# Long filters of block 2 made in eight parts between its first products, by position parity, kept in DRAM and read back

## The chip, the cores and the metric

The kernel runs on one core of a Trainium2 chip. TensorE multiplies matrices into the accumulators (PSUM), VectorE and ScalarE do the element-wise work, GpSimd (POOL) here only takes a few inverse roots, and SyncE (SP) issues the DMAs that bring weights from DRAM. The engines run side by side and meet at semaphores. The metric is the time of one execution on the device in microseconds (us), less is better.

## The reference

Two blocks are run one after the other on 256 positions of 2048 channels, in float32. The change touches the second block's mixer, and there the long filters. They depend on the weights alone, not on the input:

```python
def hyena_kernel_fft(L, fw1, fb1, freq, fw2, fb2, fw3):
    ...
    hdn = jnp.sin(freq * (feats @ fw1 + fb1))
    hdn = jnp.sin(freq * (hdn @ fw2 + fb2))
    h = (hdn @ fw3).astype(f32).reshape(L, HY_ORDER, 2, HY_W)
    ...
    h = h * jnp.exp(-t[:, :, None, None] * jnp.abs(deltas))
    k = jnp.concatenate([h[:, :, 0], jnp.zeros((1, HY_ORDER, HY_W), f32), h[:0:-1, :, 1]], axis=0)
    k = k / (jnp.sum(jnp.abs(k), axis=0, keepdims=True) + EPS)
    return jnp.fft.rfft(k, axis=0)
...
    for o, gate in enumerate(gates):
        z = gate * (fft_conv(z, kf[:, o]) + z * lp['hy_bias'][o])
```

L is 256, HY_W is 1024. `fft_conv` transforms z, multiplies by the filter's spectrum and transforms back. The kernel does the transforms as matmuls with tables of cosines and sines at the odd frequencies, since the sum of both halves of the filter gives the real part and their difference the imaginary one.

## The kernel before

Everything is float32. A weight piece is 512 x 512, arrives in two DMAs (halves of 512 KB) in one of four ring slots (`w_raw`), is split by ScalarE into a high part (`w_hi`, line 1039 in block 2) and by VectorE into the rest (`w_lo`, line 1662), and TensorE multiplies it in three passes (lines 2359 to 2361, `product2`). A product with one stream is 24 matmuls of 512 columns. Piece n can be loaded when product n - 4 is done; each engine's code splits piece n + 2 in iteration n.

Block 2 starts with the 12 chunks of its input projection (loop `for j in range(12)`). Chunks 0 to 3 are made for two streams, x and the context c. Chunk 0 has pieces 0 to 3, first with c and then with x, since x comes last out of block 1: between its products TensorE turns the normalised x (`turn_x2`), VectorE modulates it (`whole`), ScalarE rounds it (`whole_hi`) and VectorE takes the rest. Chunk 1 has products 4 to 7, chunk 2 has 8 to 11, chunk 3 (`DT`) is product 12 and the first x-only chunk starts at 13. At the end of a chunk ScalarE copies the accumulators out (line 1127) before the next chunk can write them. Between the products stand the short convolutions: TensorE turns a tile forward, ScalarE and VectorE apply the taps (`centre2`, `taps2`), TensorE turns it back. All orders are written out by hand: the order of the code of an engine is its order of work. `side` is a pair of accumulator banks and `turn` another, each handed over by a full and a free semaphore, in the order of the lists `side_uses` and `order`.

Behind the last chunk come the scan's heads (until about 2533 us of the span), its output (VectorE lines 1862 to 1872), and then, in this order on TensorE:

- the filters, for each of the two orders: the taps `h` (line 2583, 8 matmuls of 512 columns on 64 rows), their norm (line 2590, 8 matmuls with ones on `h_abs`, which ScalarE makes), and the spectra `K` of sum and difference (line 2599, 16 matmuls). VectorE applies the decay (lines 1885, 1887), sums (1890, 1892), takes the reciprocal of the norm (1906) and scales the spectra (1913);
- the convolutions, for each order and each half c of the channels: forward transform `Z` (line 2617), VectorE's product with `K` (lines 1926 to 1934), inverse transform into `side` (line 2628), and VectorE's bias, add and gate (lines 1941 to 1947). Between the first two transforms the gate rows are spread (`spread_gate`, line 2605);
- the output projection. Its weights from the third piece on are loaded when the convolutions are done, because their slots hold `hy_b`, `fw3` and `idft` until then.

## Time and profile before

| | us |
|---|---|
| median of 3 runs | 3564.24 (3562.53 to 3570.66) |
| profiled execution, its own time | 3575.23 |
| its span | 3573.4 |
| TensorE busy in the span | 3451.4 |
| VectorE busy | 2355.6 |
| ScalarE busy | 1617.9 |

The profile is one execution, recorded by the hardware. "Busy" is the time in which an engine worked on an instruction; matmuls are pipelined, so their shown durations overlap and the distance from start to start is what one costs. PEclk is the clock that TensorE was granted, as a share of 2.4 GHz; the clock has two levels, 1.2 and 2.4 GHz, so a window with 0.75 was at each for half of the time. A name such as `L2617` is the line of the kernel before. Each float32 matmul of the filters and convolutions shows as two records (x16 are 8 matmuls); those of the products are one each.

### The profile page before, as it was taken

To read this page: it belongs to the slowest core of one execution; us is meant where nothing else is said; L and a number is where in the kernel's file an instruction comes from. 1 tells how busy PE (TensorE), PEld (TensorE's weight loads), DVE (VectorE), ACT (ScalarE), POOL (GpSimd) and SP (SyncE) were. 2 spreads that over 40 slices of the span, in tenths; PEclk is the share of its full clock that TensorE was granted. 3 is DMA by queue.
4 is the path that set the end of the run, shared out by engine and by line. 5 is a ranking of instruction groups with operands and counts; after the bars stand their busy time and mean duration, and the time that the engine had idled before them with its cause. 6 is when DMAs were issued, how large, how long until landed. Compare 5 with 4: busy or idle time off the path is not lost.

```text
span 3573.4 us, 42859 instructions
## 1 busy us (share of the span) xinstructions
PE 3451.4 (97%) x15810; PEld 2810.8 (79%) x15810; DVE 2355.6 (66%) x2911; ACT 1617.9 (45%) x2131; POOL 33.4 (1%) x28
## 2 busy tenths in 40 slices
PE   7999999999999999999999999999887999999998
PEld 6888888887788888888878887878534788888887
DVE  5667888888766666777767663566655665656565
ACT  5555555555434545555554442444211543434343
POOL 0000000000000000000000000000000000000000
PEclk9999999999999999999999999999988999999999
DMA  7557777776676467777777753566002576667664
GB/s 237 151 175 221 225 220 226 227 229 213 224 238 205 142 188 227 226 226 230 231 220 256 252 173 96 155 195 195 1 0 96 160 221 201 220 200 222 201 220 157
DMA packets 357809, 687.84 MB, mean 192 GB/s; under 512 B 24591, under 2 KB 28704, under 8 KB 356384
## 3 DMA queue, kind: packets, MB, share of 16 engines
q1 hardware_dynamic: 357664, 685.82, 61.1%
q8 instruction: 101, 1.65, 0.2%
q14 instruction: 44, 0.36, 0.0%
HBM read 683.64 MB, written 2.10 MB: 192 GB/s over the span
## 4 chain that ended last, share of the span: by engine, by line
PE 69%; issue 21%; DVE 5%; ACT 2%; DMA 1%; DVEq 1%; SPq 0%; ACTq 0%; POOL 0%; POOLq 0%
PE acc L2083 16%; PE acc L2085 16%; PE acc L2084 16%; PE acc L2359 4%; PE acc L2360 4%; PE acc L2361 4%; DVE w_lo L1247 1%; DMA w_raw<-in_w_down 1%; PE turn L2290 1%; PE acc L2617 1%; PE turn L2104 1%; PE turn L2120 1%; PE acc L2583 1%; DVE ada_sum L1350 1%; PE side L2628 1%
## 5 line engine op out<-in xcount | busy, mean ns | idle before, releaser
L1247 DVE TENSOR_TENSOR w_lo<-w_raw,w_hi 128x1024 fp32r<-128x1024 f32 x708 | 838.4, 1221 | 380.4 <-ACT w_hi L771 346.2
L771 ACT ACTIVATE w_hi<-w_raw 128x1024 fp32r<-128x1024 f32 x708 | 739.0, 1062 | 718.2 <-DMA w_raw<-in_w_up 315.3
L2083 PE MATMUL acc<-w_hi,in_h 128*128 128x512 f32 x1408 | 553.0, 393 | 0.0
L2085 PE MATMUL acc<-w_hi,in_l 128*128 128x512 f32 x1408 | 548.6, 390 | 0.0
L2084 PE MATMUL acc<-w_lo,in_h 128*128 128x512 f32 x1408 | 548.0, 389 | 0.0
L2022 DVE TENSOR_TENSOR w_lo<-w_raw,w_hi 128x1024 fp32r<-128x1024 f32 x252 | 303.1, 1222 | 195.7 <-ACT w_hi L1211 187.6
L1211 ACT ACTIVATE w_hi<-w_raw 128x1024 fp32r<-128x1024 f32 x252 | 264.7, 1060 | 330.2 <-DMA w_raw<-in_w_mlp 329.8
L2359 PE MATMUL acc<-w_hi,in_h 128*128 128x512 f32 x992 | 395.9, 399 | 15.9 <-issue 6.0
L2361 PE MATMUL acc<-w_hi,in_l 128*128 128x512 f32 x992 | 390.3, 393 | 0.0
L2360 PE MATMUL acc<-w_lo,in_h 128*128 128x512 f32 x992 | 390.2, 393 | 0.0
L1350 DVE SCALAR_TENSOR_TENSOR ada_sum<-w_raw,silu_c,ada_sum 128x512 f32<-128x512 f32 x450 | 327.6, 750 | 31.7 <-issue 8.0
L2083 PEld LDWEIGHTS acc<-w_hi,in_h 128*128 128x128 f32 x1408 | 264.4, 188 | 56.2 <-issue 1.6
L2085 PEld LDWEIGHTS acc<-w_hi,in_l 128*128 128x128 f32 x1408 | 264.2, 188 | 55.6
L2084 PEld LDWEIGHTS acc<-w_lo,in_h 128*128 128x128 f32 x1408 | 264.5, 188 | 53.4
L2083 PE MATMUL acc<-w_hi,ah 128*128 128x512 f32 x704 | 278.9, 396 | 14.2 <-DVE w_lo L1247 7.5
L2084 PE MATMUL acc<-w_lo,ah 128*128 128x512 f32 x704 | 276.3, 392 | 0.0
L2085 PE MATMUL acc<-w_hi,al 128*128 128x512 f32 x704 | 276.2, 392 | 0.0
L2359 PEld LDWEIGHTS acc<-w_hi,in_h 128*128 128x128 f32 x992 | 188.6, 190 | 58.5 <-issue 17.3
L2361 PEld LDWEIGHTS acc<-w_hi,in_l 128*128 128x128 f32 x992 | 188.5, 190 | 40.3
L2360 PEld LDWEIGHTS acc<-w_lo,in_h 128*128 128x128 f32 x992 | 188.8, 190 | 38.2 <-issue 0.5
L2359 PE MATMUL acc<-w_hi,hid_h 128*128 128x512 f32 x512 | 200.4, 391 | 0.0
L2361 PE MATMUL acc<-w_hi,hid_l 128*128 128x512 f32 x512 | 199.4, 389 | 0.0
(353 smaller groups left out, 4730.1 us busy)
## 6 DMA issues: line engine op xcount, KB each, us to landing
w_raw<-in_w_up SPq DMA_DIRECT2D x352, 512.0 KB, 3.8
w_raw<-in_w_mlp SPq DMA_DIRECT2D x256, 512.0 KB, 3.7
w_raw<-in_w_in SPq DMA_DIRECT2D x200, 512.0 KB, 3.7
w_raw<-in_w_ada SPq DMA_DIRECT2D x192, 512.0 KB, 4.2
w_raw<-in_w_down SPq DMA_DIRECT2D x176, 512.0 KB, 4.8
w_raw<-in_w_o SPq DMA_DIRECT2D x64, 512.0 KB, 3.7
w_raw<-in_w_out SPq DMA_DIRECT2D x32, 512.0 KB, 3.8
x_sb<-in_x SPq DMA_DIRECT2D x1, 2048.0 KB, 7.8
```

The costliest lines, as they stand in the source:

```text
L771: nc.scalar.activation(hi[s][:, ks], raw[s][:, ks], ACT.Copy).then_inc(w_hi[s][h], 1)
L1211: nc.scalar.activation(hi[s][:, 2 * h:2 * h + 2], raw[s][:, 2 * h:2 * h + 2], ACT.Copy).then_inc(w_hi[s][h], 1)
L1247: nc.vector.tensor_tensor(lo[s][:, ks], raw[s][:, ks], hi[s][:, ks].bitcast(F32), ALU.subtract).then_inc(w_lo[s][h], 1)
L1350: a = nc.vector.scalar_tensor_tensor(ada_sum[v][:], raw[s][:, k], c, ada_sum[v][:], ALU.mult, ALU.add)
L2022: nc.vector.tensor_tensor(lo[s][:, ks], raw[s][:, ks], hi[s][:, ks].bitcast(F32), ALU.subtract).then_inc(w_lo[s][h], 1)
L2083: nc.tensor.matmul(acc[p][i][:], high(kt)[:, tok], hi[s][:, k], start=(kt == first), stop=False)
L2084: nc.tensor.matmul(acc[p][i][:], high(kt)[:, tok], lo[s][:, k], start=False, stop=False)
L2085: last = nc.tensor.matmul(acc[p][i][:], low(kt)[:, tok], hi[s][:, k], start=False, stop=(kt == final))
L2104: last = nc.tensor.transpose(tb[b][:, i * P:(i + 1) * P], src, ident[:])
L2359: nc.tensor.matmul(o, h_[:, kt, tok], wh[:, k, 0:cols], start=(kt == first), stop=False)
L2360: nc.tensor.matmul(o, h_[:, kt, tok], wl[:, k, 0:cols], start=False, stop=False)
L2361: last = nc.tensor.matmul(o, l_[:, kt, tok], wh[:, k, 0:cols], start=False, stop=(kt == final))
```

## The change

The filters no longer stand behind the scan. They are made in eight steps, of one order and 256 channels each, and each step has two visits of TensorE between products of block 2's first chunks:

- the first visit, in a slot of `FLT_A`, makes both directions' taps into the two banks of `side` (4 matmuls of 256 columns). VectorE then applies the decay and makes sum and difference (`filter_taps`). The norm's argument |a| + |b| is taken as the larger of |a + b| and |a - b|, on VectorE;
- the second visit, in a slot of `FLT_B`, makes the norm (2 matmuls, into `turn`) and the transform (4 matmuls). The positions are sorted into even and odd ones, and the frequencies into a first half and its mirror image, so one half table (`fdft`, 128 columns) gives two partial sums, and the spectrum's halves are their sum and difference, which VectorE makes (`filter_spectrum`). The order's bias is added to the real part there, so that the convolution's result needs the gate alone.

Slot -4 to -1 are behind chunk 0's products with c, slot n is behind product n. The slots are `FLT_A = [-4, -1, 2, 4, 6, 8, 10, 12]` and `FLT_B = [-3, 0, 3, 5, 7, 9, 11, 13]`. A step's spectra (0.5 MB) are stored to a DRAM tensor; when the projection's last pieces are used up, all are read back to where the weights of the ring's two free slots were, in pieces of 1 KB in a partition's row. VectorE waits for them at the first product of each order.

Also moved: the two small matmuls and sines that make `hdn` (from the chunk at product 28 on to the last down projection of block 1), the loads of `dft`, `masks` and the filter's small weights (to the same place), the modulation of x (from VectorE to ScalarE, `whole_features`), and the normalisation of the scan's output (from the middle of the filters to behind VectorE's products of the first order). Buffers were given other addresses.

The diff, cut to its core:

```diff
+    by_parity = np.concatenate([pos[0::2], pos[1::2]])
+    c["feats"] = np.concatenate([t, np.cos(f * w), -np.sin(f * w)], 1).T.astype(f32)[:, by_parity].copy()
...
+    freq = np.concatenate([pos[:P], pos[::-1][:P]])
+    ang = 2 * np.pi * ((2 * freq[None, :] + 1) * pos[:, None] % (4 * TOK)) / (4 * TOK)
+    c["fdft"] = np.stack([v[by_parity, 0:P].astype(f32).reshape(TT, P, P).transpose(1, 0, 2) for v in (np.cos(ang), np.sin(ang))], 1).copy()
...
+        def filter_load(s):
+
+            o, ch = s // 4, slice(s % 4 * FC, (s % 4 + 1) * FC)
+            sp.wait_ge(flt_taps, s)
+            w3 = t["filt_w3_2"][0].rearrange("k (o d n) -> k o d n", o=2, d=2)
+            sp.dma_start(flt_w[:], w3[:, o, :, ch]).then_inc(flt_in, 16)
+            sp.dma_start(flt_decay[:], t["decay"][:, :, ch]).then_inc(flt_in, 16)
+            sp.dma_start(flt_b[s % 2][:], t["hy_bias_2"][:, o, ch].to_broadcast([P, FC])).then_inc(flt_in, 16)
+
+        def filter_store(s):
+
+            sp.wait_ge(k_made, s + 1)
+            sp.dma_start(k_store[s, :, 0], flt_sum[:]).then_inc(k_stored, 16)
+            sp.dma_start(k_store[s, :, 1], flt_dif[:]).then_inc(k_stored, 16)
+
+        def filter_moves(n):
+
+            for s in range(8):
+                if n == max(3, FLT_A[s] + 5) and s < 7:
+                    filter_load(s + 1)
+                if n == max(3, FLT_B[s] + 5):
+                    filter_store(s)
+
+        sp.wait_ge(sin_s, 2)
+        filter_load(0)
         for j, (col, _, _) in enumerate(CHUNKS):
             if j == DT:
                 s, r = ring(FIRST[j])
...
+                sp.wait_ge(w_free[ring(OUT0 + n)[0]][h], ring(OUT0 + n)[1])
+        sp.wait_ge(k_stored, 16 * 16)
         for o in range(2):
-            sp.dma_start(fw3[o][:], t["filt_w3_2"][0][:, o * 2 * HYW:(o + 1) * 2 * HYW]).then_inc(fw3_in, 16)
-        sp.dma_start(idft[:], t["idft"]).then_inc(idft_in, 16)
+            for m in range(2):
+                for q in range(4):
+                    sp.dma_start(K[o][m][:, :, q * FC:(q + 1) * FC], k_store[4 * o + q, :, m]).then_inc(k_in, 16)
+            if o == 0:
+                sp.dma_start(idft[:], t["idft"]).then_inc(idft_in, 16)
...
+        def whole_features(names, full, dst):
+
+            for i, u in enumerate(names):
+                b, k = UNITS[u]
+                act_.wait_ge(t_full[b], k)
+                for f in range(2):
+                    kt = 2 * i + f
+                    src, s_, b_ = tb[b][:, f * TOK:(f + 1) * TOK], scale2[:, 0, kt:kt + 1], mod[:, kt, 0:1]
+                    nc.scalar.activation(full[:, kt], src, ACT.Identity, scale=s_, bias=b_)
+                    a = nc.scalar.activation(dst[:, kt], src, ACT.Identity, scale=s_, bias=b_)
+                a.then_inc(part2_hi, 1)
+                act_.drain().then_inc(t_free[b], 1)
...
+        def filter_taps(s):
+
+            for b in range(2):
+                dve.wait_ge(side_full[b], SIDE[b]["h", s] + 1)
+            two = lambda b: side[b][:].rearrange("p (t n) -> p t n", t=TT)
+            nc.vector.tensor_tensor(flt_h0[:], two(0), flt_decay[:], ALU.mult).then_inc(side_free[0], 1)
+            nc.vector.scalar_tensor_tensor(flt_q[:, 0], two(1)[:, 0], not_first[:], flt_decay[:, 0], ALU.mult, ALU.mult)
+            nc.vector.tensor_tensor(flt_q[:, 1], two(1)[:, 1], flt_decay[:, 1], ALU.mult).then_inc(side_free[1], 1)
+            dve.drain()
+            if s > 0:
+                dve.wait_ge(k_stored, 32 * s)
+            nc.vector.tensor_tensor(flt_sum[:], flt_h0[:], flt_q[:], ALU.add)
+            nc.vector.tensor_tensor(flt_dif[:], flt_q[:], flt_h0[:], ALU.subtract)
+            dve.drain()
+            nc.vector.tensor_tensor(flt_q[:], flt_sum[:], flt_dif[:], ALU.max)
+            nc.vector.tensor_tensor(flt_h0[:], flt_sum[:], flt_dif[:], ALU.min)
+            dve.drain()
+            nc.vector.scalar_tensor_tensor(flt_q[:], flt_h0[:], -1.0, flt_q[:], ALU.mult, ALU.max)
+            dve.drain().then_inc(flt_taps, 1)
+
+        def filter_spectrum(s):
+
+            b, k = UNITS["nm", s]
+            dve.wait_ge(t_full[b], k)
+            nc.vector.tensor_scalar(flt_r[:], tb[b][:, 0:FC], EPS, None, ALU.add).then_inc(t_free[b], 1)
+            dve.drain()
+            nc.vector.reciprocal(flt_r[:], flt_r[:])
+            dve.drain()
+            for m, dst in enumerate((flt_q, flt_h0)):
+                dve.wait_ge(side_full[m], SIDE[m]["dft", s] + 1)
+                nc.vector.tensor_tensor(dst[:], side[m][:].rearrange("p (t n) -> p t n", t=TT),
+                                        flt_r[:].unsqueeze(1).to_broadcast([P, TT, FC]), ALU.mult).then_inc(side_free[m], 1)
+            dve.drain()
+            nc.vector.tensor_tensor(flt_q[:, 0], flt_q[:, 0], flt_b[s % 2][:], ALU.add)
+            nc.vector.tensor_tensor(flt_dif[:, 0], flt_h0[:, 0], flt_h0[:, 1], ALU.add)
+            nc.vector.tensor_tensor(flt_dif[:, 1], flt_h0[:, 1], flt_h0[:, 0], ALU.subtract)
+            dve.drain()
+            nc.vector.tensor_tensor(flt_sum[:, 0], flt_q[:, 0], flt_q[:, 1], ALU.add)
+            nc.vector.tensor_tensor(flt_sum[:, 1], flt_q[:, 0], flt_q[:, 1], ALU.subtract)
+            dve.drain().then_inc(k_made, 1)
+
+        def filter_step(slot):
+
+            if slot in FLT_A:
+                filter_taps(FLT_A.index(slot))
+            if slot in FLT_B:
+                filter_spectrum(FLT_B.index(slot))
+
+        for i in range(8):
+            if i % 2 == 0:
+                filter_step(i // 2 - 4)
+            dve.wait_ge(part2_hi, 8 + i + 1)
+            two = slice(2 * i, 2 * i + 2)
+            nc.vector.tensor_tensor(in_l[:, two], in_f[:, two], in_h[:, two].bitcast(F32), ALU.subtract).then_inc(part2_lo, 1)
...
-            dve.wait_ge(filt_in, 16 * 8)
-            dve.wait_ge(t_full[b], k)
-            nc.vector.tensor_scalar(hdn_a[:], tb[b][0:HY_HID, 0:TOK], filt[:, i + 1:i + 2], filt[:, 0:1], ALU.add, ALU.mult).then_inc(t_free[b], 1)
-            dve.drain()
...
-            for c in range(2):
-                nc.vector.tensor_scalar(r_norm[:, c * CH:(c + 1) * CH], side[c][:], EPS, None, ALU.add).then_inc(side_free[c], 1)
-            dve.drain()
-            nc.vector.reciprocal(r_norm[:], r_norm[:])
-            dve.drain()
+            dve.wait_ge(k_in, 128 * (o + 1))
...
@@ -1935,17 +1985,19 @@
                     if m == 1:
                         a.then_inc(yf_s, 1)
                     dve.drain()
+            if o == 0:
+
+                dve.wait_ge(ssd_sq, 1)
+                nc.vector.tensor_scalar(ss2[:, 0, 0:4], ss2[:, 0, 0:4], 1.0 / 512, EPS, ALU.mult, ALU.add).then_inc(stat, 1)
+                dve.wait_ge(rstd, 19)
+                y_groups = xs[0][:].rearrange("p t (g w) -> p (t g) w", w=CH)
+                nc.vector.tensor_tensor(y_groups, y_groups, rstd2[:, 0, 0:4].unsqueeze(2).to_broadcast([P, 4, CH]), ALU.mult).then_inc(mix_s, 1)
             for c in range(2):
                 ch = slice(c * CH, (c + 1) * CH)
-                dve.drain()
-                nc.vector.tensor_tensor(hy_t[:], hy[0][:, :, ch], hy_b[:, o, ch].unsqueeze(1).to_broadcast([P, TT, CH]), ALU.mult)
-                dve.drain()
                 for i in range(TT):
                     dve.wait_ge(side_full[i], SIDE[i]["conv", o, c] + 1)
-                    nc.vector.tensor_tensor(hy_t[:, i], hy_t[:, i], side[i][:], ALU.add).then_inc(side_free[i], 1)
-                dve.drain()
-                nc.vector.tensor_tensor(hy[0][:, :, ch], hy_t[:], hy[1 + o][:, :, ch], ALU.mult).then_inc(conv_s, 1)
-                dve.drain()
+                    nc.vector.tensor_tensor(hy[0][:, i, ch], side[i][:], hy[1 + o][:, i, ch], ALU.mult).then_inc(side_free[i], 1)
+                dve.drain().then_inc(conv_s, 1)
         nc.vector.tensor_tensor(hy_sq[:], hy[0][:], hy[0][:], ALU.mult)
...
+        def filter_visit(slot):
+
+            if slot in FLT_A:
+                s = FLT_A.index(slot)
+                if s == 0:
+                    pe.wait_ge(ada_mod, 2 * ADA_LAYER + 1)
+                pe.wait_ge(flt_in, 48 * (s + 1))
+                for d in range(2):
+                    o = fill_side(d, ("h", s))
+                    for tt in range(TT):
+                        last = nc.tensor.matmul(o[:, tt * FC:(tt + 1) * FC], hdn[1][:, tt * P:(tt + 1) * P], flt_w[:, d], start=True, stop=True)
+                    last.then_inc(side_full[d], 1)
+            if slot in FLT_B:
+                s = FLT_B.index(slot)
+                pe.wait_ge(flt_taps, s + 1)
+                b = fill(("nm", s))
+                for tt in range(TT):
+                    last = nc.tensor.matmul(tb[b][:, 0:FC], masks[:, ONES], flt_q[:, tt], start=(tt == 0), stop=(tt == 1))
+                last.then_inc(t_full[b], 1)
+                for m, src in enumerate((flt_sum, flt_dif)):
+                    o = fill_side(m, ("dft", s))
+                    for tt in range(TT):
+                        last = nc.tensor.matmul(o[:, tt * FC:(tt + 1) * FC], fdft[:, m, tt], src[:, tt], start=True, stop=True)
...
+                filter_visit(n)
```

In the diff of VectorE's part the lines left out ahead of `dve.wait_ge(k_in, ...)` are the whole of the old filter code (lines 1874 to 1915), and on TensorE lines 2577 to 2600 go.

On TensorE, behind the scan's output, the rows of the kernel before end the second order's filters and come to the first convolution (`hy` is z, `dft_sb` the table):

```order
L2575 MATMUL side<-states,bcT 128x512 x8
L2583 MATMUL acc<-fw_0_243,hdn_220 128x512 x8
L2590 MATMUL side<-h_abs_201,masks_sb 128x512 x4
L2590 MATMUL side<-h_abs_202,masks_sb 128x512 x4
L2599 MATMUL acc<-h_sum,dft_sb 128x512 x4
L2599 MATMUL acc<-h_200,dft_sb 128x512 x4
```

Then come the first order's other spectra, the same once more with `fw_1`, and `L2617`. After the change the convolution stands next to the scan's output:

```order
L2654 MATMUL side<-states,bcT 128x512 x8
L2672 MATMUL acc<-hy_166,dft_sb 128x512 x8
L2660 MATMUL turn<-g_diag,masks_sb 128x128 x8
L2672 MATMUL acc<-hy_166,dft_sb 128x512 x8
L2660 MATMUL turn<-g_diag,masks_sb 128x128 x8
```

All 64 matmuls of 512 columns between the two are gone from here.

On TensorE at the end of chunk 1 (the last matmul of product 7, the turn of a convolved tile, the first of product 8), before:

```order
L2361 MATMUL acc<-w_hi_61,hc_l 128x512
L2120 MATMUL turn<-ident_sb,cvB_161 128x128 x8
L2359 MATMUL acc<-w_hi_52,in_h 128x512
L2360 MATMUL acc<-w_lo_51,in_h 128x512
L2361 MATMUL acc<-w_hi_52,in_l 128x512
```

and after, with the second visit of a step between turn and product:

```order
L2422 MATMUL acc<-w_hi_61,hc_l 128x512
L2172 MATMUL turn<-ident_sb,cvB_161 128x128 x8
L2547 MATMUL turn<-flt_q,masks_sb 128x256 x2
L2552 MATMUL side<-flt_sum,fdft_sb 128x256 x2
L2552 MATMUL side<-flt_dif,fdft_sb 128x256 x2
L2420 MATMUL acc<-w_hi_52,in_h 128x512
```

The six matmuls of the visit write neither of the accumulators of the products. The same stands ahead of products 4 and 12.

On VectorE around iteration 14 (`cvB` is a tile of the short convolution, `w_lo` the rest of a weight piece, `dt_raw` the scan's step widths), before:

```order
L1693 SCALAR_TENSOR_TENSOR cvB_160<-turn,table_92,cvB_160 128x4x63 x8
L1662 TENSOR_TENSOR w_lo_51<-w_raw_50,w_hi_52 128x1024 x2
L1702 TENSOR_TENSOR dt_raw<-side,dt_b 128x128
L1705 TENSOR_SCALAR dt_abs<-dt_raw 128x128
L1706 TENSOR_SCALAR dt_relu<-dt_raw 128x128
L1708 TENSOR_TENSOR dt_abs<-dt_abs,dt_raw 128x128
L1693 SCALAR_TENSOR_TENSOR cvB_161<-turn,table_92,cvB_161 128x255 x4
L1662 TENSOR_TENSOR w_lo_54<-w_raw_53,w_hi_55 128x1024 x2
```

and after, from behind `dt_abs` on:

```order
L1769 TENSOR_TENSOR dt_abs<-dt_abs,dt_raw 128x128
L1827 TENSOR_SCALAR flt_r<-turn 128x256
L1829 RECIPROCAL flt_r<-flt_r 128x256
L1833 TENSOR_TENSOR flt_q<-side,flt_r 128x512
L1833 TENSOR_TENSOR flt_h_198<-side,flt_r 128x512
L1836 TENSOR_TENSOR flt_q<-flt_q,flt_b_205 128x256
L1837 TENSOR_TENSOR flt_dif<-flt_h_198 128x256
L1838 TENSOR_TENSOR flt_dif<-flt_h_198 128x256
L1840 TENSOR_TENSOR flt_sum<-flt_q 128x256
L1841 TENSOR_TENSOR flt_sum<-flt_q 128x256
L1754 SCALAR_TENSOR_TENSOR cvB_161<-turn,table_92,cvB_161 128x255 x4
L1723 TENSOR_TENSOR w_lo_54<-w_raw_53,w_hi_55 128x1024 x2
```

The nine operations of the last step's spectrum stand between the step widths and the next splits, and the eight of its taps ahead of the first row of the piece before.

## Rows read from the trace of the kernel before

**Rows 1.** The page's first part: busy us, share of the span, instructions.

```profile
PE 3451.4 (97%) x15810; PEld 2810.8 (79%) x15810; DVE 2355.6 (66%) x2911; ACT 1617.9 (45%) x2131; POOL 33.4 (1%) x28
```

**Rows 2.** Windows of 2169 to 2327: us, busy by engine, PEclk, DMA share, GB/s.

```profile
2169.00:2184.00 15.00, 13.02 (x52) 10.63 (x53) 2.36 (x2) 3.77 (x6) 0.00 (x0) 0.89 0.26 72
2184.00:2220.00 36.00, 35.97 (x174) 29.89 (x172) 13.86 (x22) 11.05 (x17) 0.00 (x0) 1.00 0.31 88
2220.00:2234.00 14.00, 11.28 (x58) 9.86 (x59) 2.36 (x2) 5.11 (x10) 0.00 (x0) 0.88 0.19 47
...
2264.00:2277.00 13.00, 13.00 (x99) 11.64 (x98) 2.70 (x3) 2.29 (x4) 0.00 (x0) 0.87 0.15 42
2277.00:2327.00 50.00, 50.00 (x244) 41.52 (x243) 37.92 (x64) 28.24 (x39) 0.00 (x0) 0.97 0.66 200
```

**Rows 3.** TensorE's timeline, products: start, us, instruction [idle before <-releaser].

```profile
2170.98 0.47 PE L2359 MATMUL acc<-w_hi,in_h 128*128 128x512 f32 x1 [2.20 <-issue]
...
2222.72 0.47 PE L2359 MATMUL acc<-w_hi,in_h 128*128 128x512 f32 x1 [2.75 <-issue]
...
2263.80 0.28 PE L2375 MATMUL acc<-hc_h,w_hi 128*32 128x256 f32 x1 [2.32 <-ACT yB L1127]
...
2371.12 0.64 PE L2515 MATMUL turn<-feats_sb,fw 33*64 33x256 f32 x2
...
2380.26 0.39 PE L2359 MATMUL acc<-w_hi,in_h 128*128 128x512 f32 x1
2380.49 0.39 PE L2360 MATMUL acc<-w_lo,in_h 128*128 128x512 f32 x1
```

**Rows 4.** TensorE's timeline, filters and convolutions.

```profile
2546.55 1.98 PE L2583 MATMUL acc<-fw,hdn 64*128 64x512 f32 x4
2551.06 10.77 PE L2583 MATMUL acc<-fw,hdn 64*128 64x512 f32 x12 [2.53 <-DVE xs_x L1869]
...
2633.25 7.11 PE L2617 MATMUL acc<-hy,dft_sb 128*128 128x512 f32 x16 [1.47 <-DVE K L1913]
...
2646.93 8.74 PE L2617 MATMUL acc<-hy,dft_sb 128*128 128x512 f32 x16 [1.86 <-DVE Yt L1927]
...
2659.46 13.90 PE L2628 MATMUL side<-Yf,idft_sb 128*128 128x512 f32 x32
2673.20 7.03 PE L2617 MATMUL acc<-hy,dft_sb 128*128 128x512 f32 x16
...
2706.18 7.10 PE L2628 MATMUL side<-Yf,idft_sb 128*128 128x512 f32 x16 [3.24 <-DVE hy_t L1945]
```

**Rows 5.** Windows in the filters and at the first convolution, columns as in 2.

```profile
2551.00:2562.00 11.00, 10.94 (x13) 3.79 (x14) 6.26 (x9) 5.95 (x11) 0.00 (x0) 0.51 0.00 0
...
2633.00:2641.00 8.00, 7.75 (x24) 3.95 (x24) 1.83 (x4) 0.00 (x0) 0.00 (x0) 1.00 0.00 0
```

**Rows 6.** VectorE's timeline, filters and convolutions.

```profile
2550.32 0.69 DVE L1869 TENSOR_TENSOR xs_x<-xs_x,acc 128x512 f32<-128x512 f32 x1
...
2558.46 0.75 DVE L1885 SCALAR_TENSOR_TENSOR h<-acc,not_first_sb,decay_sb 128x512 f32<-128x512 f32 x1 [2.40 <-PE acc L2583]
...
2569.19 2.29 DVE L1900 TENSOR_TENSOR xs_x<-xs_x,rstd 128x2048 f32<-128x2048 f32 x1 [1.12 <-POOL rstd L740]
...
2572.77 6.55 DVE L1906 RECIPROCAL r_norm<-r_norm 128x1024 f32<-128x1024 f32 x1
...
2643.02 1.29 DVE L1934 TENSOR_TENSOR Yf<-Yf,Yt 128x512 f32<-128x512 f32 x2
```

**Rows 7.** VectorE's timeline, splits of weights between the products.

```profile
2129.04 2.36 DVE L1662 TENSOR_TENSOR w_lo<-w_raw,w_hi 128x1024 fp32r<-128x1024 f32 x2 [1.71 <-ACT w_hi L1039]
...
2293.33 6.99 DVE L1662 TENSOR_TENSOR w_lo<-w_raw,w_hi 128x1024 fp32r<-128x1024 f32 x6
```

**Rows 8.** DMA issues of 2400 to 2760: count, KB each, median us to landing.

```profile
w_raw<-in_w_in SPq DMA_DIRECT2D x20, 512.0 KB, 3.6
...
decay_sb<-in_decay SPq DMA_DIRECT2D x1, 1024.0 KB, 5.2
```

252 lines of the change are left out of this document (95 added, 157 removed).

## Prediction

> **What bounds the kernel now.** I read the page's busy times first: TensorE is busy for 97% of the span [rows 1]. So any TensorE time that is added between products costs its full length, and time comes back only where TensorE is removed from the chain, waits, or runs at its lower clock. The windows by stage come next [rows 2]: between the products of block 2 TensorE is busy nearly throughout (36 of 36 us from 2184 on, 50 of 50 from 2277 on), while VectorE is busy for 37.9 of the last 50 and the DMA engines at 0.66. Three windows are different: around 2169, 2220 and 2264 TensorE waits, and its granted clock is 0.89, 0.88 and 0.87, a mixture of 2.4 and 1.2 GHz. The timeline of TensorE puts a wait of 2.20, 2.75 and 2.32 us there, each at the start of a chunk, while ScalarE empties the accumulators of the chunk before [rows 3]. Last, the timeline from 2546 to 2713, where there are no weights to load [rows 4]: TensorE makes the filters from 2546.55 on, and the first matmul of the first convolution starts at 2633.25. That is a serial piece of 86.7 us in which TensorE and VectorE take turns and the clock falls again and again (0.51 from 2551 to 2562 against 1.00 from 2633 to 2641 [rows 5]). This piece is what the change moves.
>
> The sum is made against the profiled execution, 3575.23 us, and its span of 3573.4. It lies 11.0 us above the median of the three runs shown (3564.24), which I take for spread of the whole run, not of this stretch.
>
> **What is removed at the convolutions.** After the change the first convolution's forward transform stands where the filter matmuls stood. Its first half can start at 2546.55, when the first accumulator is free, and the other must wait for VectorE's last read of the second accumulator (L1869), which ends at 2551.0 [rows 4, 6]. Half of a transform is 7.11 / 2 = 3.55 us [rows 4], so it ends at 2554.6 and not at 2633.25 + 7.11 = 2640.36: 85.8 us earlier. Three things change behind it.
> - The gate's spread now waits for a diagonal that ScalarE used to have ready; I work the second transform's start out 7.1 us behind the first's end, where it was 6.57 (2646.93 less 2640.36). The main part of that wait is VectorE's, which still has to read the accumulators. Cost 0.5.
> - The normalisation of the scan's output (1.12 us of wait for GpSimd and a multiply of 2.29 [rows 6], and 0.2 for a small operation) moves behind VectorE's products for the first order and ahead of its first read of `side`. TensorE has 13.9 us of inverse transforms in one piece there [rows 4], in four quarters of 3.4, and the third needs the first one's bank: in old times VectorE's products end at 2663.5 (2646.93 + 8.74 for the transform, then eight of at most 0.69 and four of 0.65), its first read of `side` at 2663.5 + 3.6 + 0.7 = 2667.8, and the second quarter at 2659.46 + 6.9 = 2666.4. Cost 1.4.
> - The bias multiply is folded into the spectrum, so VectorE's answer to an inverse transform is one multiply of 0.69 in place of a multiply, an add and a multiply. The wait of 3.24 ahead of the last transforms [rows 4] becomes 1.8, gain 1.4, and the tail behind the last transform starts 1.3 earlier (a multiply of 512 in place of an add of 512 and a multiply of 1024, which is two of 0.65 more [rows 6]).
>
> The clock: the old rows show 0.51 right after a wait of 2.53 that followed two shorter ones, and 1.00 after a wait of 1.47 [rows 4, 5]. Here a wait of 1.0 remains and 3.5 us of work lie ahead of it. Between nothing and 3.55 us (the second half at half clock) I take 2.0. The sum at the end is -85.8 + 0.5 + 1.4 - 1.4 - 1.3 + 2.0 = **-84.6 us**.
>
> The Trainium skill, page "TensorE: Matmul & The Clock Gate", section "HAM oscillation — how this bites in real kernels", says that a matmul stream cut up by waits drops to half rate and pays for the climb at each piece. The trace agrees for the 11 us at 0.51 [rows 5]. By that rule the whole of the first transform would be at half clock, and the sum 5 us less favourable; the row with 1.00 speaks against taking it everywhere.
>
> **What is added between the products.** Each of the eight steps has two visits of TensorE: 4 matmuls of 256 columns (the taps), and 6 (2 for the norm, 4 for the transform). The transform needs fewer than before, since by parity it is made for one half of the frequencies and VectorE adds and subtracts the rest. A float32 matmul of 512 columns takes 0.859 us (16 from 2659.46 to 2673.20 [rows 4]), so one of 256 takes 0.43: 80 x 0.43 = 34.4. A visit is also a switch. The nearest row is the single 256-column matmul at 2371.12, 0.64 long against 0.43 [rows 3]; some of that overlaps, so 0.15 each between 0 and 0.21, 16 x 0.15 = 2.4. Together 36.8, with TensorE full on both sides.
>
> What it gives back: the second visits of steps 3, 5 and 7 stand exactly at the three chunk starts, each 2.58 us of work that is independent of the accumulators. They fill waits of 2.20, 2.75 and 2.32: 7.3 - 0.2 = 7.1. With the waits gone the clock should stay: (1 - 0.89) x 15 + (1 - 0.88) x 14 + (1 - 0.87) x 13 = 5.0 [rows 2]. The bounds are 0 and 12.1; I take all of it, because the rows ahead and behind stand at 1.00.
>
> What it costs in waits: VectorE's taps take 5.1 us, from 0.69 (read of 512 from PSUM), 0.40 and 0.35 for halves, four of 0.65, one of 0.75 and four drains [rows 6]; its spectrum takes 5.5, from a reciprocal of 6.55 / 4 = 1.64, two reads of 0.69, six small ones of 0.35 and drains. The second visit needs the taps of the first one, a product later. A product of 24 matmuls is 24 x 0.23 = 5.5 us [rows 3], one of 48 is 11. Walking through the engines' orders with these durations, four places come out late:
> - first step: the taps stand behind `split_lo2(3)` (2129.04 + 2.36 = 2131.4 [rows 7]), end at 2136.6, and TensorE is through with its product, its visit and the turns at 2134.8: 1.8.
> - second step: the taps wait behind the splits of x, 1.4.
> - sixth step: the short convolution's taps (eight operations on 256 columns, some 3.5) and a split (2.4) stand ahead, and the product is short, 1.2.
> - eighth step: VectorE was dense there already (6.99 us of splits in one piece [rows 7]); taps and spectrum put 10.6 us more ahead of splits that products 17 to 21 need, 1.9 net.
>
> That is 6.3; the other twelve handovers have 1 to 6 us in hand. The bounds are 0 and 8 x 2.5 = 20, if each second visit comes as late as the one at 2551 did. The sum in the products is 36.8 - 7.1 - 5.0 + 6.3 = **+31.0 us**.
>
> **At nothing:** the sine arguments and the two small matmuls move from chunk 7 to the down projection, as long there as here. The 0.25 MB of `fdft`, the 0.5 of `dft` and the 0.3 of masks are loaded during the down projection now: 1.1 MB, 5.2 us by the row of the decay [rows 8], ahead of weights that come 4 to 7 us before their product. No cost, up to 3. Modulating x goes from VectorE to ScalarE, which is idle there. 4 MB of spectra are written, 0.5 MB a step over some 22 us, beside weights at 0.3 to 0.6 of the engines: hidden. Reading 4 MB back and 0.5 of `idft` starts at 2479 as `decay` did; at 1 MB in 5.2 us it takes 23 us and has until 2554.6, 75 us. On SyncE's queue the waits for taps and spectra stand behind loads whose own slot is free later, except for the store of the last step (piece 19 behind it has 9 us in hand).
>
> **Sum:** -84.6 + 31.0 = -53.6. The profiled execution becomes 3521.6, and the median 3564.24 - 53.6 = **3510.6**. Ends: at the convolutions -87 to -79; in the products +24 to +45, as waits of 0 to 20 and the clock's 5 go together or against each other.
>
> **Rivals.**
> - *Handovers late all over.* Each second visit waits as long as the second-half wait at 2551, 2.5 us; 20 in place of 6.3: 3524. For it: VectorE gets 85 us more in 190 us of products. Against it: it was idle for over half of that. 0.20.
> - *The gaps are not filled*, since ScalarE's read comes behind other work, or the clock falls anyway: +12, 3522.5. 0.08.
> - *The convolutions run at the lower clock* with fewer matmuls around them: the first transform and the next one whole, +5 to 9, 3517. 0.07.
> - *Slower than before:* the weight loads stand on SyncE's queue behind its 16 waits for VectorE. Where such a wait is the last, TensorE sees the load's 3.6 us to landing [rows 8] and a split of 1.2 (6.99 / 6 [rows 7]): 16 x 4.8 = 77, which gives 3587. It is slower than before from 54 / 16 = 3.4 us a wait on. Against it: the code puts each wait behind a load whose slot comes later. 0.03.
> - *It doesn't do what it says:* the spectra aren't back in time. Pieces of 1 KB a row in place of 8 would have to be over 3 times slower than the row; at 4 times TensorE waits 19 us, 3529. 0.02. The Trainium skill, page "Perfetto Trace Analysis", section "DMA Optimizations", says that pieces under 2 KB have a large overhead each; no row here has such a piece in bulk.
>
> **Chances and range.** The forecast has 0.60 with 3502 to 3519 as its own range. The range is 3499 to 3530: it takes in the first three rivals and the ends of the sum. A change of 0.2% (7 us) is about what a measurement of this kernel can tell from none. Faster by more than that 0.96, within it 0.01, slower 0.03.
>
> **What would show it.** Right: the first transform ends some 50 us earlier than 2640 in the span, with no filter matmul behind the scan; the three chunk starts show no wait and a clock of 0.97 or more; taps matmuls take 1.7 us a visit. Wrong: TensorE waiting for the taps at most second visits (then the first rival), `w_hi` waiting for DMA with TensorE behind it (the fourth), or VectorE waiting for the spectra at the first convolution (the fifth).

## The result, and the profile after

The changed kernel takes 3540.57 us (median of 4 runs, 3533.33 to 3542.15) against 3563.39 of the kernel before; the ratio is 0.9928, with a 95% interval of 0.9908 to 0.9947. It is faster, by 0.7% and not by the 1.5% forecast: 22.8 us in place of 53.6, and 3540.6 lies above the range (3499 to 3530). A second set of runs, on another occasion, gave 3539.83 and 0.9926 (0.9912 to 0.9940). Of the sets further down, that of `before_warm` has two executions of 16068 and 9006 us; its ratio leaves them out, and why they were so long is not known.

The two profiled executions differ by more than the medians: the spans are 3573.4 and 3531.6 us, 41.8 apart. So of the 30.8 us by which the forecast missed the medians, 11.8 lie between the forecast and the two traces, and 19.0 between the traces and the medians. Both parts have to be explained.

TensorE's busy time falls by 38.7 us and VectorE's rises by 17.5 (the page's first part, beside [rows 1]):

```profile
PE 3412.7 (97%) x15842; PEld 2807.7 (80%) x15842; DVE 2373.1 (67%) x2981; ACT 1619.6 (46%) x2146; POOL 33.5 (1%) x28
```

The windows of the changed kernel, from the first product of block 2 to the scan in three stretches, then from the first convolution to the out products (us, busy time by engine, granted clock, DMA share, GB/s; beside [rows 2, 5]):

```profile
2118.70:2294.70 176.00, 165.99 (x812) 137.64 (x813) 111.17 (x177) 58.99 (x98) 0.70 (x1) 1.00 0.37 105
2294.70:2353.70 59.00, 55.08 (x290) 45.42 (x289) 45.77 (x81) 23.20 (x33) 0.00 (x0) 0.94 0.50 155
2353.70:2516.90 163.20, 162.99 (x763) 132.69 (x761) 112.33 (x131) 79.51 (x104) 0.00 (x0) 1.00 0.66 204
...
2586.00:2682.10 96.10, 69.88 (x178) 32.88 (x176) 52.61 (x78) 14.34 (x38) 3.91 (x2) 0.88 0.06 22
```

In the products TensorE computes for 384 of 398 us; in the convolutions for 70 of 96. None of its waits below is ended by a DMA.

TensorE's timeline at the visits (start, us, instruction, in brackets the wait ahead of it and what ended it; each matmul of a visit is two records here, each of a product one):

```profile
2124.38 1.99 PE L2540 MATMUL side<-flt_w,hdn 64*128 64x256 f32 x8
2126.30 0.50 PE L2420 MATMUL acc<-w_hi,hc_h 128*128 128x512 f32 x1
...
2161.09 1.10 PE L2547 MATMUL turn<-flt_q,masks_sb 128*128 128x256 f32 x4 [1.71 <-ACTq L871]
...
2182.31 1.02 PE L2547 MATMUL turn<-flt_q,masks_sb 128*128 128x256 f32 x4
...
2184.71 0.58 PE L2420 MATMUL acc<-w_hi,in_h 128*128 128x512 f32 x1
...
2213.41 1.10 PE L2547 MATMUL turn<-flt_q,masks_sb 128*128 128x256 f32 x4 [2.62 <-DVE cvB L1754]
...
2242.31 1.10 PE L2547 MATMUL turn<-flt_q,masks_sb 128*128 128x256 f32 x4 [0.34 <-ACT xs_ctx L1118]
...
2317.70 1.26 PE L2547 MATMUL turn<-flt_q,masks_sb 128*128 128x256 f32 x4 [2.61 <-DVE cvB L1754]
...
2321.97 2.07 PE L2552 MATMUL side<-flt_dif,fdft_sb 128*128 128x256 f32 x4 [1.31 <-DVE dt_raw L1763]
```

A first visit takes 1.9 us (2124.38 to 2126.30), a second one 2.4 where it doesn't wait (2182.31 to 2184.71). At the three old chunk starts, where TensorE waited 2.20, 2.75 and 2.32 [rows 3], it now waits 0 (at 2182), 0.34 (at 2242) and 0.34 (at 2292). But the visits of steps 4, 6 and 8, which stand right behind the forward turns of the short convolution, wait 2.62, 2.62 and 2.61, and step 8 waits once more.

The waits in sum, from the groups by line between 2118.7 and 2516.9 (count | busy, mean ns | idle time ahead and what ended it):

```profile
L2540 PE MATMUL side<-flt_w,hdn 64*128 64x256 f32 x64 | 15.9, 389 | 0.0
...
L2547 PE MATMUL turn<-flt_q,masks_sb 128*128 128x256 f32 x32 | 8.9, 401 | 12.6 <-DVE cvB L1754 7.9 <-DVEq L1821 2.4 <-ACTq L871 1.7
...
L2552 PE MATMUL side<-flt_dif,fdft_sb 128*128 128x256 f32 x32 | 9.3, 416 | 1.3 <-DVE dt_raw L1763 1.3
```

12.6 + 1.3 = 13.9 us of waits, where the prediction had 6.3. VectorE's timeline names the holder of the bank:

```profile
2211.45 3.73 DVE L1754 SCALAR_TENSOR_TENSOR cvB<-turn,table,cvB 128x255 f32<-128x255 f32 x8 [3.10 <-ACT cvB L1106]
...
2321.64 0.28 DVE L1763 TENSOR_TENSOR dt_raw<-side,dt_b 128x128 f32<-128x128 f32 x1
```

The eight additions of the short convolution (`taps2`) read the two transposition banks (`turn`) that those forward turns have written, once ScalarE has made its part (`cvB L1106`). The second visit needs the first of them for its norm, which is free once half of the eight are done, at 2211.45 + 1.86 = 2213.3: there TensorE starts. The read of the step widths (2321.64) frees the second side bank.

The convolutions, TensorE's timeline:

```profile
2585.97 3.60 PE L2672 MATMUL acc<-hy,dft_sb 128*128 128x512 f32 x8
2590.57 3.70 PE L2672 MATMUL acc<-hy,dft_sb 128*128 128x512 f32 x8 [1.00 <-DVE xs_x L1963]
2597.60 1.31 PE L2660 MATMUL turn<-g_diag,masks_sb 128*128 128x128 f32 x8 [3.33 <-ACT g_diag L1197]
...
2602.69 8.30 PE L2672 MATMUL acc<-hy,dft_sb 128*128 128x512 f32 x16
...
2623.62 7.10 PE L2683 MATMUL side<-Yf,idft_sb 128*128 128x512 f32 x16 [1.80 <-DVE hy L1999]
...
2644.27 9.75 PE L2672 MATMUL acc<-hy,dft_sb 128*128 128x512 f32 x16 [6.68 <-DVE Yt L1977]
...
2662.79 8.80 PE L2683 MATMUL side<-Yf,idft_sb 128*128 128x512 f32 x16 [1.90 <-DVE hy L1999]
...
2682.06 0.76 PE L2420 MATMUL acc<-w_hi,in_h 128*128 128x512 f32 x1 [1.89 <-DVE in_l L2014]
```

VectorE's timeline there, its first read of the spectra:

```profile
2594.38 0.69 DVE L1976 TENSOR_TENSOR Yf<-acc,K 128x512 f32<-128x512 f32 x1 [1.48 <-PE acc L2672]
```

VectorE waits for TensorE there and not for the readback. The DMAs of the readback (count, KB each, median us to landing):

```profile
K<-k_store SPq DMA_DIRECT2D x16, 256.0 KB, 6.8
```

They are issued from 2517.2 to 2527.3 and the slowest took 7.9, so all spectra are back at 2535.2 at the latest, 59 us before that read. The 4.5 MB with `idft` took 18 us, where the prediction had 23.

### The profile page after: what moved, and what is told of

Its sections match the earlier page's. It is cut to its first block, busy times and chain, and to the rows that moved or that the text cites. A ratio compares the mean times of both kernels' runs of the same rounds, so it can differ in the third digit from the quotient of the medians.

```text
span 3531.6 us, 43131 instructions
## 1 busy us (share of the span) xinstructions
PE 3412.7 (97%) x15842; PEld 2807.7 (80%) x15842; DVE 2373.1 (67%) x2981; ACT 1619.6 (46%) x2146; POOL 33.5 (1%) x28
## 4 chain that ended last, share of the span: by engine, by line
PE 67%; issue 21%; DVE 5%; ACT 2%; DMA 2%; DVEq 2%; SPq 0%; ACTq 0%; POOL 0%; POOLq 0%
PE acc L2135 16%; PE acc L2137 16%; PE acc L2136 16%; PE acc L2420 3%; PE acc L2422 3%; PE acc L2421 3%; DMA w_raw<-in_w_down 2%; DVE w_lo L1286 2%; PE turn L2342 1%; PE turn L2156 1%; DVE ada_sum L1389 1%; PE acc L2672 1%; PE turn L2172 1%; ACT w_hi L803 1%; DVEq L1381 1%
## 5 line engine op out<-in xcount | busy, mean ns | idle before, releaser
L2135 PE MATMUL acc<-w_hi,ah 128*128 128x512 f32 x704 | 278.0, 395 | 13.9 <-DVE w_lo L1286 8.4
```

The source lines that it names most:

```text
L2135: nc.tensor.matmul(acc[p][i][:], high(kt)[:, tok], hi[s][:, k], start=(kt == first), stop=False)
```

## The experiments

The medians of a set of runs are compared with those of the kernel before in the same set (3567.08, 3567.10 and 3564.72 in the three sets).

### Both kernels again

The traces disagreed with the medians, so both kernels were profiled twice more without a change.

> The kernel before, unchanged, for its run-to-run spread and a second trace. The two first traces differ by 41.9 us, the medians by 22.8 us, and the traces agree within 1.2 us ahead of block 2's products and behind the convolutions. Theory A (TensorE's clock inside the changed stretch differs from run to run): median 3563 to 3565, and the new trace, if it is shorter than the first one of 3573.4 us, is shorter in the stretch between 2119 and 2725 and shows there fewer or shorter pieces at the lower granted clock. Theory B (the first trace was long elsewhere): the stretch between 2119 and 2725 is again 605 us long and the new trace is shorter in the up and down projections.

> A third trace of the kernel before. Its filter piece, 86.7 and 76.7 us long in the first two, and the convolutions behind it, 91.8 and 95.6: theory (the clock is drawn anew in each run): the sum lies between 170 and 180, the waits are the same as in the others, only the matmuls' durations differ. Rival (the second trace was the exception): 86 and 92 again.

> The changed kernel, unchanged. Median 3540 (3533 to 3542). Theory A: the new trace is 3538 to 3541 us long, and the 6 to 9 us that it is longer than the first one lie in the products of block 2's first chunks or in the convolutions, where the granted clock falls to half behind waits of 1.7 to 2.6 us that left it at 1.00 in the first trace. Theory B: they lie elsewhere.

> A third trace of the changed kernel. From its first product in block 2 to the scan 398.2 and 403.5 us in the first two, from the first convolution to the out products 96.1 in both. Theory: 398 to 404 again, with the waits of 2.62 at the second visits of steps 4, 6 and 8, and 96.1.

Medians: 3565.67 (11 runs, 3559.04 to 3570.30) and 3539.83 (5 runs, 3536.94 to 3540.28). The table goes by landmarks of TensorE's timeline, in us:

| | before, three traces | mean | after, three traces | mean | difference |
|---|---|---|---|---|---|
| start to first product of block 2 | 2119.7, 2114.6, 2116.5 | 2116.9 | 2118.7, 2120.9, 2121.6 | 2120.4 | +3.5 |
| to the end of the products | 359.1, 358.9, 357.6 | 358.5 | 398.2, 403.5, 400.5 | 400.7 | +42.2 |
| scan | 67.8, 69.2, 69.1 | 68.7 | 69.1, 67.7, 69.1 | 68.6 | -0.1 |
| filter piece | 86.7, 76.7, 78.0 | 80.5 | none | | |
| first convolution to out products | 91.8, 95.6, 91.8 | 93.1 | 96.1, 96.1, 96.1 | 96.1 | -77.5 (with the filter piece) |
| rest | 848.4, 849.0, 848.4 | 848.6 | 849.5, 850.3, 849.5 | 849.8 | +1.2 |

The differences add up to -30.7. The medians say -22.8 in the first set and -27.2 in the second; without the first trace of either kernel the spans differ by 25.0. Three traces of each are few, and a difference of 3 us between such means is not much.

The first trace of the kernel before is the odd one, in the filter piece. Windows of the filter piece and of the convolutions, first trace of the kernel before:

```profile
2546.60:2633.20 86.60, 75.22 (x129) 29.67 (x128) 52.71 (x51) 12.40 (x20) 1.01 (x1) 0.78 0.00 0
2633.20:2725.00 91.80, 67.31 (x176) 32.41 (x177) 54.65 (x78) 10.11 (x26) 2.90 (x1) 0.89 0.07 23
```

The same in the second trace:

```profile
2542.70:2619.30 76.60, 64.55 (x129) 26.07 (x128) 52.65 (x51) 12.41 (x20) 1.01 (x1) 0.89 0.00 0
2619.30:2714.90 95.60, 70.40 (x176) 33.19 (x176) 54.60 (x78) 10.09 (x26) 2.90 (x1) 0.86 0.06 22
```

The granted clock was 0.78 in the one and 0.89 in the other, with VectorE's busy time the same to 0.1 us. TensorE's timeline, filter matmuls of the second order, first trace (those of the first order took 10.77 for 12 rows [rows 4]):

```profile
2590.96 12.86 PE L2583 MATMUL acc<-fw,hdn 64*128 64x512 f32 x16 [1.38 <-DVE K L1913]
```

The second trace, the same matmuls and the norm's behind them:

```profile
2585.37 7.13 PE L2583 MATMUL acc<-fw,hdn 64*128 64x512 f32 x16 [1.38 <-DVE K L1913]
2592.43 7.13 PE L2590 MATMUL side<-h_abs,masks_sb 128*128 128x512 f32 x16
```

7.13 for 16 rows is 0.43 each and some 0.2 at the end: the full clock. The third trace has a filter piece of 78.0, so the rival that the second trace was the exception falls. Theory A holds: the execution on which the largest term rested was one of several possible, and a long one. Of 54 more executions of this kernel, over three sets, only one was longer than its 3575.23 us. In the changed kernel theory A holds as well: of the 6.9 us that its second trace is longer than its first, 5.3 lie in the products, at a granted clock of 0.97 in place of 1.00 up to the last visit.

### The two halves apart

`novisit`: TensorE's and VectorE's filter work between the products is gone, the convolutions are those of the change.

```diff
         def filter_visit(slot):
-            if slot in FLT_A:
...
+            pass
...
         def filter_spectrum(s):
-            b, k = UNITS["nm", s]
...
             dve.drain().then_inc(k_made, 1)
```

> The changed kernel without TensorE's and VectorE's work on the filters between the products: a constant is stored and read back as the spectra, all DMAs of the filters stay. Left is the gain at the convolutions and the cost of the DMAs. If the gain of the traces (82.4 us from the scan to the out products) holds in the median: 3563.4 - 82.4 = 3481, and the work between the products then costs 3540.6 - 3481 = 59.6, with 20 more than the 39.1 of the trace. If the first trace of the kernel before was longer than usual in that stretch by its 11 us: 3563.4 - 71.4 = 3492, and the work between the products costs 48.6. If the DMAs of the filters or the readback cost something, it shows here as a wait of the products or of the first convolution, and the time is longer by that.

3496.54 us (ratio 0.9804, 0.9791 to 0.9818). The convolutions' side of the change, with the few us that changed ahead of block 2 and at the end, is worth 70.5 us in the median. That is nearer to the second branch (3492) than to the first traces (3481); the work between the products costs 3539.83 - 3496.54 = 43.3, where the prediction had 31.0. Its products take 359.2 us, where the kernel before has 357.6 to 359.1: the DMAs of the filters alone delay them little or not at all.

`before_nofilt`: the kernel before, whose loop over the two orders of filters is left out on TensorE, VectorE and ScalarE.

```diff
-        for o in range(2):
-            for i in range(4):
-                p = take(("h", o, i))
...
+        for m in range(2):
+            nc.vector.memset(K[0][m][:], 1.0)
```

> The kernel before without the making of the filters behind the scan (a constant is written as the spectra; the bias multiply and the short path through the convolutions are kept, the normalisation of the scan's output stands where the change has it). The difference to the kernel before is what the serial piece costs in the median. The first trace had 86.7 us for it, the second 76.7, with the same instructions: 16 filter matmuls took 12.86 us in the one and 7.13 in the other. Theory (TensorE's granted clock in this piece differs from run to run, the first trace was an unlucky one): the median is 3567 - 75 = 3492, the piece is worth 73 to 78. Rival (86.7 is what it is worth, and the gain was lost in the new convolution stretch): 3480.

3498.20 us (0.9809, 0.9796 to 0.9822), 68.9 less, and above both forecasts. Its trace has 104.2 us from the first convolution to the out products, where the three traces before have 93.1 in the mean, since the fills and the gate's spread now stand on the path; with these 11 the piece is worth about 80, the mean of the three traces. 86.7 as the usual worth would need 3480. The two ends of that estimate are from different executions, so 80 is good to some 4 us.

### What the second visits wait for

`pevisit`: VectorE's filter arithmetic is left out.

```diff
         def filter_spectrum(s):
             b, k = UNITS["nm", s]
             dve.wait_ge(t_full[b], k)
-            nc.vector.tensor_scalar(flt_r[:], tb[b][:, 0:FC], EPS, None, ALU.add).then_inc(t_free[b], 1)
...
+            dve.sem_inc(t_free[b], 1)
```

> The changed kernel with VectorE's arithmetic on the filters left out (some 85 us of it in the eight steps): it only waits for each visit of TensorE and frees the banks, and constants are stored as spectra. TensorE's 16 visits and all DMAs stay as they are. Theory (TensorE's waits at the second visits, 13.6 us in the first trace, are for the transposition bank that the short convolution and ScalarE hold, and for the step widths' side bank, not for VectorE's filter work): only the taps' part in step 1 goes, 3539. Rival (handovers late because VectorE has too much to do, the first rival of the prediction): the waits go, 3540 - 13 = 3527.

3540.45 us, the time of the changed kernel (0.9928, 0.9912 to 0.9944). The waits are all there (TensorE's timeline):

```profile
2216.76 1.10 PE L2527 MATMUL turn<-flt_q,masks_sb 128*128 128x256 f32 x4 [2.62 <-DVE cvB L1754]
...
2322.66 1.10 PE L2527 MATMUL turn<-flt_q,masks_sb 128*128 128x256 f32 x4 [2.61 <-DVE cvB L1754]
...
2326.93 2.08 PE L2532 MATMUL side<-flt_dif,fdft_sb 128*128 128x256 f32 x4 [1.73 <-DVE dt_raw L1763]
```

Only the wait of step 1 for the taps, 2.35 in the first trace of the changed kernel, is 1.72 here, for the bank. VectorE is busy for 78.0 us less than in the changed kernel (2295.1 against 2373.1), and the time is the same. So the added work on VectorE costs nothing in this kernel's time, and the prediction's first rival falls. What is left as the cause is the order in which banks are handed out, and the next run tests it.

`dftfirst`: in the second visit the four transform matmuls come first, with a semaphore of their own, the two of the norm last.

```diff
             if slot in FLT_B:
                 s = FLT_B.index(slot)
-                pe.wait_ge(flt_taps, s + 1)
-                b = fill(("nm", s))
+                pe.wait_ge(flt_two, s + 1)
                 for m, src in enumerate((flt_sum, flt_dif)):
...
+                pe.wait_ge(flt_taps, s + 1)
+                b = fill(("nm", s))
```

> The changed kernel with the second visit turned round: the four transform matmuls first, which need only the sum and the difference (with a semaphore of their own), the norm's two last, which need a transposition bank. Theory (in the trace the second visits of steps 4, 6 and 8 wait 2.62 us for the bank that the short convolution's additions on VectorE free, that of step 2 1.71 for ScalarE's read of the bank, and that of step 1 2.35 for the taps): the 1.7 us of transform matmuls fill these waits, 1.7 each in steps 2, 4 and 6, 2.1 in step 1, nothing in step 8, where the second side bank comes late as well. Together 7.3: median 3533. Rival (the visits wait for VectorE's taps as the prediction had it, and the bank only comes last by chance): 2.1 from step 1 alone, 3538.

3533.06 us (0.9910, 0.9897 to 0.9924), 6.8 less than the changed kernel. The theory had 7.3 and its rival 2.1. 0.89 is left of the 2.62 in step 4, 0.91 in step 6, and nothing in steps 1 and 2. Step 8 waits longer, 6.02 in one piece in place of 2.61 and 1.31 (TensorE's timeline):

```profile
2210.90 1.10 PE L2554 MATMUL turn<-flt_q,masks_sb 128*128 128x256 f32 x4 [0.89 <-DVE cvB L1755]
...
2315.04 2.07 PE L2549 MATMUL side<-flt_dif,fdft_sb 128*128 128x256 f32 x4 [6.02 <-DVE dt_raw L1764]
```

`step8` puts this one visit three products later, and its bank at another place in the order.

```diff
-    FLT_B = [-3, 0, 3, 5, 7, 9, 11, 13]
+    FLT_B = [-3, 0, 3, 5, 7, 9, 11, 16]
...
-    NM_AFTER = {("F", 0, "c"): 3, ("B", 0, "c"): 4, ("F", 1, "c"): 5, ("B", 1, "c"): 6, ("F", 2, "x"): 7}
+    NM_AFTER = {("F", 0, "c"): 3, ("B", 0, "c"): 4, ("F", 1, "c"): 5, ("B", 1, "c"): 6, ("F", 2, "c"): 7}
```

> dftfirst with the second visit of the eighth step three slots later (from the product of slot 13 to that of slot 16). In dftfirst that visit waited 6.02 us for VectorE's read of the step widths in the second side bank, which stands behind the short convolution and a split, and the clock fell behind it. Theory: 6.0 and 1 to 2 of clock come back: 3533 - 7.5 = 3526. Rival (the wait covers VectorE's own lateness, which comes out at the next product): 3531 to 3533.

3526.72 us (0.9886, 0.9872 to 0.9900), 6.3 less. The visit doesn't wait any more, but a later product does, for a split of its weights, and runs at half clock behind it (TensorE's timeline):

```profile
2345.69 0.80 PE L2421 MATMUL acc<-w_hi,in_h 128*128 128x512 f32 x1 [2.98 <-DVE w_lo L1724]
```

Both theories had a part. The theory had 7.5 us to gain: by the medians 1.2 of them are missing, by the two traces, which differ by 4.3 us, 3.2. This wait is the one place seen where VectorE's load does reach TensorE.

### The clock in the waits

`warm` is `step8` with seven kinds of waits, from the first convolution to the out products, filled with matmuls whose results nobody reads (some 55 in the window below; the lines shown hold one of the places).

```diff
+        def warm(n, out):
+            for _ in range(n):
+                nc.tensor.matmul(out[:, 0:TOK], masks[:, ONES], dft[:, 0, 0], start=True, stop=True)
...
+                if (o, c) == (1, 1):
+                    warm(15, tb[fill(("ssd", 0))])
```

> step8 with filler matmuls (256 columns, results unused) in the waits from the first convolution to the out products: 2 in the wait of 1.00, 7 in that of 3.33, 4 in those of 1.94 and 1.80, 15 in that of 6.68, 12 in that of 5.74, 3 in that of 1.89. In the trace of the changed kernel transforms of 7.03 us at full clock took 8.30, 9.75 and 8.80, and some ten of the first out matmuls ran at half clock: 8 to 10 us in all. Theory (these waits let the clock fall): step8 less 8, 3518. Rival (the clock does not follow the fillers, or they hold up what they stand ahead of): step8 or up to 5 more.

3516.41 us (0.9861, 0.9847 to 0.9876), 10.3 less than `step8`. Windows from the first convolution to the out products, `step8`:

```profile
2577.90:2674.00 96.10, 69.86 (x178) 32.98 (x176) 52.69 (x78) 14.32 (x38) 3.90 (x2) 0.88 0.06 22
```

The same in `warm`:

```profile
2577.90:2667.50 89.60, 86.44 (x288) 49.61 (x286) 52.55 (x78) 14.28 (x38) 3.91 (x2) 1.00 0.07 24
```

TensorE's timeline in `warm`, the transform behind the longest wait and the one after it:

```profile
2633.66 6.68 PE L2683 MATMUL acc<-hy,dft_sb 128*128 128x512 f32 x15 [0.21 <-DVE Yt L1978]
...
2640.60 7.03 PE L2696 MATMUL side<-Yf,idft_sb 128*128 128x512 f32 x16
```

96.1 us at 0.88 become 89.6 at 1.00, and the transform that took 9.75 takes 6.9 again (2633.66 to 2640.60). From the first out product to the turns of x it is 52.2 in place of 55.2. So the waits are what let the clock fall in this stretch: with them filled it stays at 1.00.

`warm2` adds fillers ahead of block 2, ahead of the second half of the out products and ahead of the MLP.

```diff
+        warm(6, acc[take(("in", 0, "c"))][0])
...
+                if (m, i) == (1, 2):
+                    warm(3, fill_side(0, "root"))
...
                 turn_branch(1)
+                warm(7, side[0])
```

> warm with filler matmuls in five more waits: 6 in that of 3.0 ahead of the first product of block 2, 3 and 7 in those of 1.40 and 3.23 ahead of the second half of the out products, 6, 3 in those of 2.70 and 1.42 ahead of the MLP (its wait of 4.32 is left). In the trace of warm the matmuls behind the first two ran at half clock for some 3 us each. Theory (a filled wait keeps the clock): 1.5 to 2.6, 1.5 and up to 2 us come back, 3516.4 - 5 = 3511. Rival (the fillers cost instruction fetch or come at a wrong place, as in before_warm, where the stretch behind was 8 us longer): 3517 to 3525.

3510.10 us (0.9845, 0.9827 to 0.9862), the fastest kernel here, 54.6 us less than before. The theory had 3511. Its median is 6.3 below that of `warm`, but against the kernel before in the same set it gains 3.9 on it (54.6 and 50.7); so these fillers are worth 4 to 6 us, less surely than the first ones. That `warm2` comes to the time forecast for the change is chance: by the ratios some 29 us of it are edits that the change doesn't have.

`before_warm` tried the same in the filter piece of the kernel before.

```diff
+                if i == (2, 0)[o]:
+                    warm((5, 3)[o], spare)
                 p = take(("h", o, i))
...
+                    if (c, m) == (1, 0):
+                        warm(6, spare)
```

> The kernel before with filler matmuls (256 columns, 0.43 us each, results unused, into a free transposition bank) in the waits of the filter piece: 5 in the wait of 2.53, 6 in those of 3.46 and 2.59 (and their first-order twins), 3 in those of 1.38 and 1.47. They fit into the waits at full clock. Theory (the waits let the clock fall, and that makes the piece long and uneven): 128 rows of 0.43 and 11 us of waits are 66 to 68 us in place of 77 and 87; median 3557, and the runs lie closer together than the 12 us of the kernel before. Rival (the clock falls for another reason): 3567 or a little more.

3576.06 us (ratio 1.0025, 1.0016 to 1.0035), where the theory had 3557 and its rival 3567 or a little more: both missed. The filter piece took 77.1 us, as in the second trace, and not 66 to 68. The fillers for the wait of 2.53 stood one group of matmuls behind it, so it was not filled, and behind the six others TensorE still waited 2.39 for VectorE. The other 8 us were lost far behind the edit, in the MLP: 4.9 in two waits that no other engine ended, which no trace of the kernel before has, and most of the rest in matmuls at half clock behind them (TensorE's timeline; the first row is the wait for VectorE):

```profile
2577.78 3.10 PE L2608 MATMUL acc<-h_sum,dft_sb 128*128 128x512 f32 x4 [2.39 <-DVE K L1913]
...
3016.05 0.58 PE L2360 MATMUL acc<-w_lo,in_h 128*128 128x512 f32 x1 [2.56 <-issue]
...
3200.29 0.58 PE L2360 MATMUL acc<-w_lo,in_h 128*128 128x512 f32 x1 [2.29 <-issue]
```

Why TensorE waits there stays open. So what the clock alone costs in the filter piece was not isolated. That its time differs from run to run with the clock is shown by the three traces; that filling its waits would hold it is not.

## Why the prediction was wrong, point by point

In sum, over three traces of each kernel: the convolutions' side gave 77.5 in place of 84.6, and the products cost 42.2 in place of 31.0. Outside both 4.6 us were added where the sum has nothing.

**The filter piece, -85.8.** The first step that failed. The mechanism was right: the first transform starts behind the last matmul of the scan (2585.97), its second half waits 1.00 and it ends at 2594.27, 8.3 us later, where the prediction had 8.1 (2546.55 to 2554.6). What was mis-sized is what was taken away. The text itself showed a clock of 0.51 in it and then priced the piece at the length of that one execution, 86.7. Over three traces it is 80.5. With the convolutions behind it the removed stretch is 173.5 in the mean and was 178.5 in the first trace: 5.0 of the 7.1 missing us.

**The convolutions behind it.** Against the first trace itself the gain is 82.4, 2.2 short of 84.6. The third quarter waits 1.80 (forecast 1.4), the last transforms 1.90 (forecast 1.8). The gate's spread cost more: 8.4 us from the end of the first transform to the second (2594.27 to 2602.69), not 7.1, since the diagonals come late twice (waits of 3.33 and 1.94; the first trace of the kernel before has one of 1.94). The tail is 10.6 in place of 11.9: 1.3, as said.

The clock's 2.0 came out in size and not in place. After the change two transforms and the last inverse one take more than 6.9 us from start to end, by 1.3, 2.7 and 1.7 (8.30, 9.75 and 8.80 shown). The first trace of the kernel before has two such, 1.7 (8.74 [rows 4]) and 2.2:

```profile
2686.82 9.26 PE L2617 MATMUL acc<-hy,dft_sb 128*128 128x512 f32 x16 [6.59 <-DVE Yt L1927]
```

The net cost is 1.8. But the first transform, for which the 2.0 was set, ran at full clock in both halves (3.60 and 3.70), ahead of its wait of 1.00 and behind it.

**The visits, 36.8.** Right in kind, 1.6 low. A first visit costs 1.9 and 0.1 on either side, a second one 2.4 and 0.3: 8 x 2.1 + 8 x 2.7 = 38.4.

**Waits at the handovers, 6.3.** The second step that failed, and the largest in the products: 13.9 measured, at other places for another reason. Step 1 waited for the taps in one trace (2.35) and for ScalarE's read of the bank in the others (1.71), step 2 for ScalarE (1.71), steps 4, 6 and 8 for the bank (2.6 each), steps 5 and 7 for ScalarE (0.34 each), and step 8 once more for the side bank (1.31). The walk through the engines followed the semaphore of the taps and not the second condition of the same visit, `fill(("nm", s))`: the unit ahead of it in the bank's turn is read by eight additions of VectorE, some 3.7 us. The prediction knew those additions ("some 3.5") and counted them against step 6 alone. Of the four late places that it named, steps 1 and 2 come out near in size (1.8 and 1.4 forecast). Step 6 is late by accident, by 2.62 and not 1.2, and step 8 by 3.9 and not 1.9. Step 4 was not named.

**What the gaps give back, 7.1 + 5.0.** The waits were filled (7.3 less 0.7), as forecast. The clock is the third step that failed: 5.0 was to come back. By parts the products should cost 38.4 + the waits - 7.3 - 1.3 for the two small matmuls moved out of chunk 7. With waits of 13.9, 13.6 and 13.1 that is 43.7, 43.4 and 42.9 in the three traces, and measured were 39.1, 44.6 and 42.9, trace by trace in the table's order. So 4.6 us came back in the first trace, in the second 1.2 more were lost, in the third it was nothing: 1.1 in the mean. The clock is at 0.94 in the window from 2294.7 and at 0.97 in the products of the second trace, and behind the new waits of 2.61 and 1.31 at 2318 and 2322 four rows of a visit took 2.07. To take the whole of 0 to 12.1 needed that no new wait arises, and the same text listed four.

**At nothing.** Readback, stores and the loads of the filters were hidden, as said. The stretch ahead of block 2 became 3.5 us longer, where "up to 3" stood as the bound; 1.3 of it are the two moved matmuls (0.64 each), for the rest no run was made, and the traces of one kernel differ by up to 5.1 us there, so the cause stays open. Nothing was set for the 1.2 behind.

**From the profile to the median.** The prediction took the 11.0 us that the profiled execution had over the median for spread outside this stretch. Some 7 of them lay in it (filter piece and convolutions together 178.5, against 172.3 and 169.8 in the other two traces). What the change removes had been long in just that execution, and the median doesn't hold that excess, so it can't be subtracted from it.

**The rivals.** Of those named none is the cause. "Handovers late all over" had waits of 20 and the text 6.3, with 13.9 measured between them, and its reason, VectorE's load, was refuted by `pevisit`. "The gaps are not filled, or the clock falls anyway" was right in its second half only. "The convolutions run at the lower clock" did not occur as said: the first transform ran at full clock, and the net cost was 1.8. The slower rival and the one on the readback did not occur. The sizes of the first three together, which the text never added, are 3510.6 + 13.7 + 12 + 6.4 = 3542.7: the range left out the case in which several come true at once. That the sum is near the measured 3540.6 is chance, since these were not the causes.

The Trainium skill, page "TensorE: Matmul & The Clock Gate", section "HAM oscillation — how this bites in real kernels", describes for a kernel whose waits for DMAs are longer than the work between them how such waits lower the clock. Most waits here are shorter than the work between them, and the traces agree in kind: 0.88 with the waits and 1.00 with fillers in them. What the prediction worked out from it, the first transform at half clock, did not come.

## What to carry to other kernels

A stretch in which TensorE waits often had no fixed length here: before pricing its removal, read it in several executions, or price its matmuls at full clock and give the clock a range of its own. When independent work is put into a gap, follow every buffer that it takes to its last reader, not only the data that it needs; here turning two parts of a visit round gave 6.8 us. And where short waits can't be removed, matmuls that nobody reads, into a free bank, can hold the clock; but they have to be measured: 10.3 us here for the first set of them and 4 to 6 for the second, and a loss in `before_warm`.

## What the runs showed of the chip that was not expected

- The same instructions in the same order took 86.7, 76.7 and 78.0 us in three executions; 16 rows of filter matmuls took 12.86 or 7.13 us.
- Filler matmuls held the granted clock at 1.00 over 89.6 us in which it had been 0.88.
- With some twenty matmuls more in the program (`before_warm`), in the one trace of it, TensorE waited 2.56 and 2.29 us for nothing that the profile shows, 400 to 600 us behind the edit, in code that was the same.
